# Modulation chunks beside attention: from a matrix product on TensorE to row blocks summed on VectorE and GpSimd

## The chip, the cores and the metric

The kernel runs on one NeuronCore of a Trainium2 chip. Times are device microseconds (us) of one execution. The engines are PE (TensorE; PEld is its weight load), DVE (VectorE), ACT (ScalarE), POOL (GpSimd) and SP (SyncE, which here only issues DMAs). All data are float32.

## What is computed

A diffusion backbone of two layers over 256 context tokens and 1024 latent tokens. Each layer scales, shifts and gates its activations by a modulation vector of 6 x 1024 numbers. It depends on a conditioning vector, and there are two of these: one for the context tokens and one for the latents.

```
mod_ctx = (silu(c_ctx) @ w_ada[l] + b_ada[l])[None, None, :]
xp, ckv, kpe = layer_step(xp, mod_ctx, None, None, None, p)
mod_lat = (silu(c) @ w_ada[l] + b_ada[l])[:, None, :]
xs, _, _ = layer_step(xs, mod_lat, rope, cache_ckv[:, l], cache_krope[:, l], p)

def layer_step(x, mod, rope, ctx_ckv, ctx_krope, p):
    sh1, sc1, g1, sh2, sc2, g2 = jnp.split(mod, 6, axis=-1)
    h = rmsnorm(x, p['norm1_g']) * (1 + sc1) + sh1
    mix, ckv, kpe = token_mixers(h, rope, ctx_ckv, ctx_krope, p)
    x = x + g1 * mix
    h = rmsnorm(x, p['norm2_g']) * (1 + sc2) + sh2
    x = x + g2 * expert_choice_ffn(h, p)
```

`token_mixers` holds attention (4 heads), a short convolution and a gated mixing of chunks; `expert_choice_ffn` is a mixture of 16 experts. `w_ada` is 2 x 1024 x 6144, 48 MB in all, and every number of it is read once. The change concerns `silu(c) @ w_ada + b_ada` and nothing else.

## The kernel before

**Chunks.** `w_ada` is worked in chunks of 512 columns, twelve to a layer, each a 1024 x 512 block of 2 MB that lies in the SBUF as 128 partitions x 8 row blocks (k) x 512. The first four chunks of layer 0 are done ahead of everything else. The other twenty are done inside attention: `ADA_ITEMS` names twelve for the attention of layer 0 (eight of layer 0, four of layer 1) and eight for that of layer 1.

**Attention.** One engine program each for PE, ACT and DVE walks over NI = 18 items, in two groups of nine. Each group (a pair of heads) has one item for the context tokens (items 0 and 9, called prompt items) and eight for tiles of 128 latent tokens. Iteration n of the loop computes scores of item n and finishes item n-1:
- PE: `scores` (L890) and `rotary_scores` (L902) of item n; `turn` (L939), four transposes of the exponents of item n-1 into PSUM bank 6; `times_values` (L957, or L954 for a prompt item); `turn_out` (L973). The order is written out by hand.
- DVE: `copy_turned` (L1636) takes each four transposes out of bank 6, six times per iteration (twice where item n-1 is a prompt item); PE may not refill bank 6 before it has. In between stand `invert_sum` (L1645), `scale_out` (L1657) and `row_max` (L1623, then L1627) for both heads of the pair.
- ACT: `exponents` (L1331) and `copy_out` (L1343).

In the text, copy (s, r) is `copy_turned` of head s, round r, so that an iteration has copies (0,0), (0,1), (0,2), (1,0), (1,1), (1,2). A slot m is the place for a chunk in iteration m+1.

**A chunk inside attention.** Chunk i stands in slot i, that is one in each of the first iterations. In the iteration, ahead of the last `times_values`, PE does `modulation` (L915): `cond` holds the two conditions in 2 of 32 columns, and for each of 8 row blocks and 4 column blocks of 128 there is one product with a 128x32 stationary block, 32 instructions. The sum stands in four row groups of bank 6. DVE adds the bias (`bias_modulation`, L1679), PE turns the result (`turn_modulation`, L924), and DVE copies it into `mod_all` (`copy_modulation`, L1688). The bias step waits until PE has summed and comes after `row_max(n, 1)` in DVE's order. The next transposes into bank 6 wait for the copy.

**Transfers.** The weights of a chunk alternate between two of the three 2 MB slots of `ring` (`ada_w[i % 2]`: slots 2 and 0). SP issues the load of chunk i (L505, and four small bias loads L507) once the bias step of chunk i-2 is done. Four chunks (`ADA_GATES`) are also stored to DRAM by POOL, eight small DMAs each (L602). Apart from these POOL has nothing to do until attention ends. `W_OUT`, the weights of the output projection (L1059), goes into the same two ring slots after the last two chunks are summed.

## Time and profile before

| | us |
|---|---|
| median of 3 runs | 2655.22 (2654.74 to 2655.59) |
| profiled execution, its time | 2650.42 |
| its span in the trace | 2648.7 |
| attention of layer 0, about | 340 to 662 |
| attention of layer 1, about | 1633 to 1950 |
| PE busy | 2418.7 (91%) |
| DVE busy | 799.2 (30%) |
| POOL busy | 224.9 (8%) |

The profile is of one execution. The busy times say how much an engine did, not what set the end; that is read from the chain of waits and, inside attention, from the order in time. A row of the timeline gives start, duration, engine, line and operation, and in brackets how long the engine sat idle before it and what ended that. A PE instruction on float32 has two records. Matmul ends are modelled and weight loads overlap matmuls, so that distances between starts are better read than ends.

### The profile page before, as it was taken

The page shows a single profiled execution, that of the slowest core. Times are in us where ns is not written, and L with a number is a line of the kernel's source. Part 1 is how long each engine was busy: PE and PEld are TensorE (multiplying, and loading weights), DVE is VectorE, ACT ScalarE, POOL GpSimd, SP SyncE. Part 2 cuts the span into 40 slices and gives each one's busy share as a digit, 9 for nine tenths or more (in the row PEclk, how much of TensorE's full clock was granted, in tenths as well). Part 3 has the DMA queues.
Part 4 walks back from the last instruction along what each step waited for, and adds up shares of the span by engine and source line. Part 5 has one row for each costly group of instructions (what it writes and reads, how often), then busy time and mean ns, then how long its engine had stood idle before and what let it go on. Part 6 is the DMA issues. An engine that isn't in the chain of part 4 may idle for free.

```text
span 2648.7 us, 33684 instructions
## 1 busy us (share of the span) xinstructions
PE 2418.7 (91%) x13939; PEld 1624.9 (61%) x13939; DVE 799.2 (30%) x1694; ACT 490.0 (18%) x985; POOL 224.9 (8%) x357
## 2 busy tenths in 40 slices
PE   3999999999995699999979999999999929999994
PEld 2545566666442587878745455676654418787873
DVE  1401344454235311111132023444533351111112
ACT  2410121122233011010142002122213401001012
POOL 1000010100000112121200000010000001212120
PEclk8999999999998799999989999999999959999997
DMA  8100213311234388888840003330023238888886
GB/s 298 43 0 20 80 66 127 129 64 42 78 122 151 123 268 280 278 269 276 276 142 16 20 0 98 110 118 11 1 90 111 88 119 263 281 277 270 275 280 232
DMA packets 164733, 383.64 MB, mean 145 GB/s; under 512 B 14610, under 2 KB 25116, under 8 KB 164636
## 3 DMA queue, kind: packets, MB, share of 16 engines
q1 hardware_dynamic: 145180, 332.68, 36.7%
q0 software_dynamic: 19456, 49.59, 7.4%
q8 instruction: 70, 1.15, 0.2%
q14 instruction: 27, 0.22, 0.0%
HBM read 334.63 MB, written 47.61 MB: 144 GB/s over the span
## 4 chain that ended last, share of the span: by engine, by line
PE 90%; DVE 5%; DMA 2%; SPq 1%; ACT 1%; issue 1%; DVEq 0%; POOL 0%; POOLq 0%; ACTq 0%
PE PS L1193 11%; PE PS L1200 11%; PE PS L1059 10%; PE PS L1220 9%; PE PS L797 8%; PE PS L957 7%; PE PS L890 6%; PE PS L751 5%; PE PS L740 5%; PE PS L939 4%; PE PS L902 4%; PE PS L1214 2%; PE PS L851 1%; PE PS L915 1%; PE PS L1178 1%; DVE top_i L1789 1%
## 5 line engine op out<-in xcount | busy, mean ns | idle before, releaser
L1193 PEld LDWEIGHTS PS<-r,ring 128*128 128x128 f32 x2048 | 285.8, 192 | 18.6 <-issue 18.6
L1193 PE MATMUL PS<-r,ring 128*128 128x160 f32 x2048 | 288.0, 302 | 3.4 <-ACT r L1436 3.4
L1059 PE MATMUL PS<-ring,mix 128*128 128x512 f32 x640 | 287.3, 603 | 1.2 <-DVE mix L1666 1.2
L1200 PE MATMUL PS<-r,ring 128*128 128x160 f32 x2048 | 283.4, 299 | 0.0
L1200 PEld LDWEIGHTS PS<-r,ring 128*128 128x128 f32 x2048 | 279.9, 190 | 0.0
L1220 PE MATMUL PS<-ring,r 128*128 128x512 f32 x512 | 228.3, 599 | 0.0
L890 PE MATMUL PS<-lat,r 128*128 128x512 f32 (+1 forms) x416 | 205.5, 579 | 5.4 <-ACT r L1316 2.7
L797 PE MATMUL PS<-r,ring 128*128 128x512 f32 (+1 forms) x576 | 208.4, 521 | 1.6 <-ACT r L1273 1.6
L1059 PEld LDWEIGHTS PS<-ring,mix 128*128 128x128 f32 x640 | 120.2, 193 | 140.8 <-issue 140.7
L957 PE MATMUL PS<-r 128*128 128x128 f32 x1536 | 202.2, 276 | 0.0
L957 PEld LDWEIGHTS PS<-r 128*128 128x128 f32 x1536 | 188.1, 192 | 18.9 <-issue 18.7
L1861 DVE TENSOR_TENSOR r<-r,PS 128x320 f32<-128x320 f32 x64 | 31.2, 488 | 505.0 <-PE PS L1200 505.0
L1636 DVE COPY r<-PS 128x512 f32<-128x512 f32 x200 | 138.3, 692 | 136.4 <-PE PS L939 135.2
L797 PEld LDWEIGHTS PS<-r,ring 128*128 128x128 f32 x576 | 109.1, 190 | 100.6 <-issue 95.0
L1220 PEld LDWEIGHTS PS<-ring,r 128*128 128x128 f32 x512 | 94.6, 190 | 120.3 <-issue 120.3
L939 PEld LDWEIGHTS PS<-ident,r 128*128 128x128 f32 x800 | 92.8, 141 | 105.5 <-issue 81.3
L1331 ACT ACTIVATE r<-PS,nmax 128x1536 f32<-128x1536 f32 x64 | 98.6, 1540 | 228.8 <-DVE nmax L1627 184.2
L751 PE MATMUL PS<-ring,r 128*128 128x512 f32 x320 | 140.0, 592 | 0.0
L939 PE MATMUL PS<-ident,r 128*128 128x128 f32 x800 | 122.2, 275 | 5.8 <-DVE r L1636 3.5
L740 PE MATMUL PS<-ring,r 128*128 128x448 f32 x320 | 123.9, 540 | 0.3 <-ACT r L1249 0.3
L1436 ACT ACTIVATE r<-PS,mod_all,scale_all 128x128 f32<-128x128 f32 x136 | 51.1, 456 | 376.1 <-PE PS L1178 376.1
L1447 ACT ACTIVATE r<-PS 128x320 f32<-128x320 f32 x64 | 24.5, 435 | 485.4 <-PE PS L1193 485.4
(254 smaller groups left out, 2199.1 us busy)
## 6 DMA issues: line engine op xcount, KB each, us to landing
ring<-in_w_gate_dram SPq DMA_DIRECT2D x32, 2048.0 KB, 9.9
ring<-in_w_up_dram SPq DMA_DIRECT2D x32, 2048.0 KB, 10.3
ring<-in_w_down_dram SPq DMA_DIRECT2D x32, 2048.0 KB, 9.5
ring<-in_w_ada_dram SPq DMA_DIRECT2D x21, 2048.0 KB, 22.9
x_dram<-r SPq DMA_DIRECT2D x20, 512.0 KB, 2.8
r<-x_dram SPq DMA_DIRECT2D x20, 512.0 KB, 4.1
ring<-in_w_in_dram SPq DMA_DIRECT2D x4, 2048.0 KB, 11.3
r<-in_x_sample_dram SPq DMA_DIRECT2D x16, 512.0 KB, 4.3
```

The source lines that it names most:

```text
L740: ins = pe.matmul(psum(4 + t % 2, 448), hT[:, k, t * P:(t + 1) * P], W_IN[0][:, k, :], start=(k == 0), stop=(k == KD - 1))
L751: ins = pe.matmul(psum(t % 4, 512), hT[:, k, t * P:(t + 1) * P], W_IN[1][:, k, :], start=(k == 0), stop=(k == KD - 1))
L797: ins = pe.matmul(psum(base + j, tn), W_IN[u][:, k, c0:c0 + P], hT[:, k, t0:t0 + tn], start=(k == 0), stop=(k == KD - 1))
L890: ins = pe.matmul(psum(3 * slot + c, w), QA[:, 2 * ITEMS[n][0] + slot, q], CKV[:, keys], start=(slot == 0), stop=(slot == 1))
L902: ins = pe.matmul(psum(3 * slot + c, w), QP[rows, ITEMS[n][0], q], KR[rows, keys], start=(slot == 1), stop=(slot == 0))
L939: ins = pe.transpose(PS[:, 6, j * P:(j + 1) * P], Pr[slot][:, (4 * r + j) * P:(4 * r + j + 1) * P], ident[:, :])
L957: ins = pe.matmul(PS[:, 7, slot * 256:slot * 256 + P], PTr[slot][:, k, :], CKVT[:, PT + k, :], start=(k == 0), stop=(k == 11))
L1059: ins = pe.matmul(psum(2 * (s % 2) + n, 512), mix[:, k, s * P:(s + 1) * P], W_OUT[n][:, k, :], start=(k == 0), stop=(k == KD - 1))
L1193: ins = pe.matmul(PS[:, b // 2, (b % 2) * 256:(b % 2) * 256 + SLOTS], W_G[:, k, b * P:(b + 1) * P], XST[par][:, k, :], start=(k == 0), sto ...
L1200: ins = pe.matmul(PS[:, 2 + b // 2, (b % 2) * 256:(b % 2) * 256 + SLOTS], W_U[:, k, b * P:(b + 1) * P], XST[par][:, k, :], start=(k == 0), ...
L1220: ins = pe.matmul(psum(4 + n, 512), HID[:, k, 0:CAP_S], W_D[:, k, n * 512:(n + 1) * 512], start=(k == 0), stop=(k == 3))
L1636: dve.tensor_copy(PTr[slot][:, 4 * r:4 * r + 4, :], psum(6, 512).rearrange("p (k q) -> p k q", q=P))\
```

## The change

- A chunk's product is split. For the context condition (g = 0) DVE sums, for the latent condition (g = 1) POOL sums: over the 8 row blocks k, acc[g] += c_t[:, column of (g, k)] * w[:, k, :], elementwise on 128 x 512. What is left to do is the sum over the 128 partitions, and PE does it with a stationary block `pick` that has ones in column g: 2 x 4 products in place of 8 x 4.
- DVE does 8 instructions per chunk, one TENSOR_SCALAR and seven SCALAR_TENSOR_TENSOR, placed between the copies of the iteration in which PE sums the chunk. POOL does 15, eight TENSOR_SCALAR and seven TENSOR_TENSOR, each waiting for the one before, as early as the weights have landed and chunk i-2 has been summed.
- The accumulators and a scratch row lie in `lat[:, 0:2560]`, where the query latents were; POOL waits for the last reader of these (`qa_summed`).
- The chunks no longer stand in one iteration after another. `ADA_SLOT` spreads them: slots 1, 2, 3, 5, 6, 8, 9, 10, 12, 13, 15, 16 in layer 0, and 1, 3, 5, 7, 9, 11, 13, 15 in layer 1. With them move the bias step, the transpose and copy, the loads and the loads of `W_OUT`.
- POOL's stores of chunk i come after its sums of chunk i+1.
- Two semaphores are dropped by merging them with others (`wrs_ready`, `ident_zero`).

```diff
+ADA_SLOT = [{i * (NI - 1) // len(items) + 1: i for i in range(len(items))} for items in ADA_ITEMS]
...
-        cond = r1[:, 9472:9728].rearrange("p (k c) -> p k c", k=KD)
+        pick = r1[:, 9472:9536].rearrange("p (g c) -> p g c", g=2)
+        scaled = lat[:, 2048:2560]
+        acc = [[lat[:, 1024 * i + 512 * g:1024 * i + 512 * (g + 1)] for g in range(2)] for i in range(2)]
...
-                for i, (la, n) in enumerate(ADA_ITEMS[l]):
+                def accumulate(i):
+                    before = (ADA_AT[l] + i) * (2 * KD - 1)
+                    pool.wait_ge(ada_landed[i % 2], 80 * ((ADA_AT[l] + i) // 2 + 1))
+                    if i >= 2:
+                        pool.wait_ge(ada_summed, ADA_AT[l] + i - 1)
+                    a = acc[i % 2][1]
+                    for k in range(KD):
+                        if k:
+                            pool.wait_ge(acc_pool, before + 2 * k - 1)
+                        pool.tensor_scalar(scaled if k else a, ada_w[i % 2][:, k, :], c_t[:, KD + k:KD + k + 1], None, ALU.mult)                            .then_inc(acc_pool, 1)
+                        if k:
+                            pool.wait_ge(acc_pool, before + 2 * k)
+                            pool.tensor_tensor(a, a, scaled, ALU.add).then_inc(acc_pool, 1)
...
+                pool.wait_ge(qa_summed, at(l, HEADS, HEADS))
+                for i in range(len(ADA_ITEMS[l])):
+                    accumulate(i)
+                    if i:
+                        store_gate(i - 1)
+                store_gate(len(ADA_ITEMS[l]) - 1)
...
-                    pe.wait_ge(ada_landed[i % 2], 80 * ((ADA_AT[l] + i) // 2 + 1))
-                    pe.wait_ge(pt_ready, at(l, ROUNDS, turned(i, 1, rounds_of(i) - 1)))
-                    for k in range(KD):
+                    pe.wait_ge(acc_pool, (ADA_AT[l] + i + 1) * (2 * KD - 1))
+                    pe.wait_ge(acc_dve, (ADA_AT[l] + i + 1) * KD)
+                    pe.wait_ge(pt_ready, at(l, ROUNDS, turned(m, 1, rounds_of(m) - 1)))
+                    for g in range(2):
                         for j in range(4):
-                            ins = pe.matmul(PS[32 * j:32 * j + 32, 6, 0:P], cond[:, k, :],
-                                            ada_w[i % 2][:, k, P * j:P * (j + 1)], start=(k == 0), stop=(k == KD - 1))
+                            ins = pe.matmul(PS[32 * j:32 * j + 32, 6, 0:P], pick[:, g, :], acc[i % 2][g][:, P * j:P * (j + 1)],
+                                            start=(g == 0), stop=(g == 1))
...
+                def accumulate(m, k0, k1):
...
+                    for k in range(k0, k1):
+                        w, col = ada_w[i % 2][:, k, :], c_t[:, k:k + 1]
+                        if k == 0:
+                            ins = dve.tensor_scalar(a, w, col, None, ALU.mult)
+                        else:
+                            dve.wait_ge(acc_dve, (ADA_AT[l] + i) * KD + k)
+                            ins = dve.scalar_tensor_tensor(out=a, in0=w, scalar=col, in1=a, op0=ALU.mult, op1=ALU.add)
```

On DVE, the stretch of an iteration of layer 0 from copy (0,0) to the first `row_max` reads before (here iteration 8, which holds chunk 7):

```order
L1636 COPY r<-PS 128x512 [waits o_summed,p_turned] x3
L1645 RECIPROCAL pinv<-psum_row 128x1 [waits exp_done]
L1657 TENSOR_SCALAR r<-PS,pinv 128x128 [waits o_turned,o_summed,dve_own]
L1636 COPY r<-PS 128x512 [waits o_summed,p_turned] x2
L1623 TENSOR_REDUCE pmax<-PS 128x1 [waits summed0]
```

and now, in an iteration that holds a chunk (here iteration 7, slot 6, chunk 4):

```order
L1669 COPY r<-PS 128x512 [waits o_summed,p_turned]
L1728 TENSOR_SCALAR lat<-ring,c_t 128x512 [waits ada_summed,ada_landed0]
L1669 COPY r<-PS 128x512 [waits o_summed,p_turned]
L1731 SCALAR_TENSOR_TENSOR lat<-ring,c_t,lat 128x512 [waits acc_dve]
L1669 COPY r<-PS 128x512 [waits o_summed,p_turned]
L1731 SCALAR_TENSOR_TENSOR lat<-ring,c_t,lat 128x512 [waits acc_dve]
L1678 RECIPROCAL pinv<-psum_row 128x1 [waits exp_done]
L1731 SCALAR_TENSOR_TENSOR lat<-ring,c_t,lat 128x512 [waits acc_dve,dve_own]
L1731 SCALAR_TENSOR_TENSOR lat<-ring,c_t,lat 128x512 [waits acc_dve] x3
L1690 TENSOR_SCALAR r<-PS,pinv 128x128 [waits o_turned,o_summed]
L1669 COPY r<-PS 128x512 [waits o_summed,p_turned]
L1731 SCALAR_TENSOR_TENSOR lat<-ring,c_t,lat 128x512 [waits acc_dve]
```

The copies and the scaling are the same; the eight sums stand between them, five of them in one run ahead of the scaling L1690.

On POOL, from the clearing of the bias rows to the loads of the gates, where before there were only stores:

```order
L595 MEMSET r 128x128 [waits conv_summed]
L596 MEMSET r 128x128
L602 DMA mod_dram<-r 16x1x8 [waits ada_biased]
L602 DMA mod_dram<-r 16x1x8 x7
L602 DMA mod_dram<-r 16x1x8 [waits ada_biased]
L602 DMA mod_dram<-r 16x1x8 x7
```

now the sums of the next chunk come ahead of each store (the last product and sum of chunk 1, the stores of chunk 0, the start of chunk 2):

```order
L611 TENSOR_SCALAR lat<-ring,c_t 128x512 [waits acc_pool]
L614 TENSOR_TENSOR lat<-lat 128x512 [waits acc_pool]
L623 DMA mod_dram<-r 16x1x8 [waits ada_biased]
L623 DMA mod_dram<-r 16x1x8 x7
L611 TENSOR_SCALAR lat<-ring,c_t 128x512 [waits ada_summed,ada_landed0]
L611 TENSOR_SCALAR lat<-ring,c_t 128x512 [waits acc_pool]
L614 TENSOR_TENSOR lat<-lat 128x512 [waits acc_pool]
```

Each of POOL's sums waits for the one before it.

On PE, at the end of an iteration with a chunk, before:

```order
L890 MATMUL PS<-lat,r 128x512
L957 MATMUL PS<-r 128x128 x4
L915 MATMUL PS<-ring,r 32x128 x32
L957 MATMUL PS<-r 128x128 x4
L924 MATMUL PS<-ident,r 128x128
```

and now:

```order
L918 MATMUL PS<-lat,r 128x512
L988 MATMUL PS<-r 128x128 x4
L945 MATMUL PS<-lat,r 32x128 x8
L988 MATMUL PS<-r 128x128 x4
L955 MATMUL PS<-ident,r 128x128
```

The place is the same; 32 instructions have become 8.

## Rows read from the trace of the kernel before

**Rows 1.** The page: engines' busy time, the chain that ended last by engine.
```profile
PE 2418.7 (91%) x13939; PEld 1624.9 (61%) x13939; DVE 799.2 (30%) x1694; ACT 490.0 (18%) x985; POOL 224.9 (8%) x357
...
PE 90%; DVE 5%; DMA 2%; SPq 1%; ACT 1%; issue 1%; DVEq 0%; POOL 0%; POOLq 0%; ACTq 0%
```

**Rows 2.** Groups by line, layer 0's attention: records, busy us, mean ns, idle.
```profile
L915 PE MATMUL PS<-ring,r 128*32 128x128 f32 x768 | 23.5, 274 | 0.0
```

**Rows 3.** Timeline, ends of iterations with a chunk: start, us, engine, line.
```profile
357.48 0.28 DVE L1679 TENSOR_TENSOR r<-PS,r 128x128 f32<-128x128 f32 x1
357.82 0.14 PEld L924 LDWEIGHTS PS<-ident,r 128*128 128x128 f32 x1 [0.69 <-DVE r L1679]
...
374.18 1.95 PE L915 MATMUL PS<-ring,r 128*32 128x128 f32 x64
375.40 0.15 DVE L1627 TENSOR_SCALAR nmax<-pmax 128x1 f32<-128x1 f32 x1
376.07 1.16 PE L957 MATMUL PS<-r 128*128 128x128 f32 x8
376.20 0.29 DVE L1679 TENSOR_TENSOR r<-PS,r 128x128 f32<-128x128 f32 x1 [0.65 <-PE PS L915]
376.52 0.39 SPq L505 DMA_DIRECT2D ring<-in_w_ada_dram  x1
376.95 0.14 PEld L924 LDWEIGHTS PS<-ident,r 128*128 128x128 f32 x1
378.67 0.69 DVE L1636 COPY r<-PS 128x512 f32<-128x512 f32 x1 [0.92 <-PE PS L939]
...
397.55 0.69 DVE L1636 COPY r<-PS 128x512 f32<-128x512 f32 x1 [0.92 <-PE PS L939]
```

**Rows 4.** Timeline, DVE in an iteration without a chunk, and the next one's first copy.
```profile
610.34 0.69 DVE L1636 COPY r<-PS 128x512 f32<-128x512 f32 x1 [0.64 <-PE PS L939]
611.85 0.69 DVE L1636 COPY r<-PS 128x512 f32<-128x512 f32 x1 [0.81 <-PE PS L939]
614.04 0.69 DVE L1636 COPY r<-PS 128x512 f32<-128x512 f32 x1 [1.50 <-PE PS L939]
619.03 0.35 DVE L1657 TENSOR_SCALAR r<-PS,pinv 128x128 f32<-128x128 f32 x1 [4.23 <-PE PS L957]
619.40 0.69 DVE L1636 COPY r<-PS 128x512 f32<-128x512 f32 x1
620.91 0.69 DVE L1636 COPY r<-PS 128x512 f32<-128x512 f32 x1 [0.81 <-PE PS L939]
...
627.04 0.69 DVE L1636 COPY r<-PS 128x512 f32<-128x512 f32 x1 [0.64 <-PE PS L939]
```

**Rows 5.** Groups by line and shape, DVE: elementwise work from SBUF to SBUF.
```profile
L1507 DVE TENSOR_SCALAR r<-r,rstd 128x1024 f32<-128x1024 f32 x20 | 15.1, 754 | 0.7
L1583 DVE SCALAR_TENSOR_TENSOR r<-mix,vec_all,r 128x1023 f32<-128x1023 f32 x4 | 5.1, 1278 | 0.0
L1583 DVE SCALAR_TENSOR_TENSOR r<-mix,vec_all,r 128x255 f32<-128x255 f32 x4 | 1.9, 484 | 0.1
```

**Rows 6.** Groups by line and shape, POOL: one input, and waits between.
```profile
L636 POOL COPY r<-r 128x256 f32 x32 | 12.8, 400 | 484.3 <-PE PS L1178 484.3
L570 POOL TENSOR_SCALAR_AFFINE_SELECT sel<-sel 128x16 f32<-128x16 f32 x4 | 0.8, 196 | 0.4
```

**Rows 7.** Stretches after the load at 376.52: us, engines, PEclk, DMA share, GB/s.
```profile
383.00:384.00 1.00, 1.00 (x6) 0.52 (x7) 0.12 (x2) 0.00 (x0) 0.00 (x0) 1.00 0.78 270
384.00:385.00 1.00, 1.00 (x8) 0.41 (x6) 0.00 (x0) 0.00 (x0) 0.00 (x0) 1.00 0.00 0
```

**Rows 8.** Timeline, DVE where a prompt item is finished (layer 0, iteration 1).
```profile
347.74 0.61 DVE L1657 TENSOR_SCALAR r<-PS,pinv 128x128 f32<-128x128 f32 x2 [1.25 <-PE PS L954]
351.89 0.69 DVE L1636 COPY r<-PS 128x512 f32<-128x512 f32 x1 [3.54 <-PE PS L939]
```

**Rows 9.** Timeline: the first products with `W_OUT` in layer 0.
```profile
662.86 7.11 PE L1059 MATMUL PS<-ring,mix 128*128 128x512 f32 x16 [0.61 <-DVE mix L1666]
```

More of the change, by code:

```diff
@@ L289, in backbone @@
         ada_summed = sem("ada_summed")
+        acc_dve = sem("acc_dve")
+        acc_pool = sem("acc_pool")
         ada_biased = sem("ada_biased")
@@ L935, in turn @@
                         pe.wait_ge(o_copied, at(l, NI, n))
-                    if slot == 0 and r == 0 and 0 < n <= len(ADA_ITEMS[l]):
-                        pe.wait_ge(ada_copied, ADA_AT[l] + n)
+                    if slot == 0 and r == 0 and n - 1 in ADA_SLOT[l]:
+                        pe.wait_ge(ada_copied, ADA_AT[l] + ADA_SLOT[l][n - 1] + 1)
                     for j in range(4):
@@ L1605, in rotate @@
                     dve.tensor_tensor(x, x, SHUF, ALU.add).then_inc(qp_ready, 1)
-                condition(cond)
+                step(dve.memset(pick, 0.0))
+                for g in range(2):
+                    ins = dve.tensor_scalar(pick[:, g, g:g + 1], ones[:, 0:1], 1.0, None, ALU.mult)
+                ins.then_inc(cond_ready, 1)
                 dve.wait_ge(wa_summed, at(l, 1, 1))
@@ L1666, in copy_value_heads, with bias_modulation @@
                     dve.tensor_copy(mix[:, h, t0:t0 + tn], psum(m % 6, tn)).then_inc(uvh_copied[1], 1)
-                def bias_modulation(i):
-                    if i < 0 or i >= len(ADA_ITEMS[l]):
+                def bias_modulation(m):
+                    i = ADA_SLOT[l].get(m)
+                    if i is None:
                         return
-                    stored = [ADA_AT[m] + k for m in range(DEPTH) for k, (_, n) in enumerate(ADA_ITEMS[m])
-                              if n in ADA_GATES and ADA_AT[m] + k <= ADA_AT[l] + i - 2 and k % 2 == i % 2]
+                    stored = [ADA_AT[q] + k for q in range(DEPTH) for k, (_, n) in enumerate(ADA_ITEMS[q])
+                              if n in ADA_GATES and ADA_AT[q] + k <= ADA_AT[l] + i - 2 and k % 2 == i % 2]
                     if stored:
@@ L1679, in bias_modulation, with copy_modulation @@
                     dve.tensor_tensor(ada_s[i % 2], psum(6, P), ada_b[i % 2], ALU.add).then_inc(ada_biased, 1)
-                def copy_modulation(i):
-                    if i < 0 or i >= len(ADA_ITEMS[l]):
+                def accumulate(m, k0, k1):
+                    i = ADA_SLOT[l].get(m)
+                    if i is None:
+                        return
+                    a = acc[i % 2][0]
+                    if k0 == 0:
+                        dve.wait_ge(ada_landed[i % 2], 80 * ((ADA_AT[l] + i) // 2 + 1))
+                        if i >= 2:
+                            dve.wait_ge(ada_summed, ADA_AT[l] + i - 1)
+                    for k in range(k0, k1):
[5 more added lines that the diff above has]
+                            ins = dve.scalar_tensor_tensor(out=a, in0=w, scalar=col, in1=a, op0=ALU.mult, op1=ALU.add)
+                        ins.then_inc(acc_dve, 1)
+                def copy_modulation(m):
+                    i = ADA_SLOT[l].get(m)
+                    if i is None:
                         return
@@ L1698, in _ @@
                 for n in range(NI):
-                    for r in range(3):
-                        copy_turned(n - 1, 0, r)
+                    copy_turned(n - 1, 0, 0)
+                    accumulate(n - 1, 0, 1)
+                    copy_turned(n - 1, 0, 1)
+                    accumulate(n - 1, 1, 2)
+                    copy_turned(n - 1, 0, 2)
+                    accumulate(n - 1, 2, 3)
                     invert_sum(n - 1, 0)
+                    accumulate(n - 1, 3, 7)
                     scale_out(n - 1, 0)
                     copy_turned(n - 1, 1, 0)
+                    accumulate(n - 1, 7, 8)
                     copy_turned(n - 1, 1, 1)
```

29 lines of the change are left out of this document (15 added, 14 removed).

## The prediction

> **What bounds the kernel now.** I read the page first. PE is busy 91% of the span and carries 90% of the chain that ended last [rows 1]. So work taken off PE counts, as far as PE does not then wait for others. The chunks stand in two attention stages. There I read the order in time, since what matters is which wait ends last within one iteration. Two distances give the frame. From first copy to first copy an iteration with a chunk takes 397.55 - 378.67 = 18.88 us [rows 3], and one without takes 627.04 - 610.34 = 16.70 us [rows 4]. A chunk costs 2.18 us of the path, twenty chunks 43.6 us; no form of this change can save more. PE has no long idle stretch in either. But PE fills bank 6 six times per iteration, and DVE must empty it each time: where rows 4 show DVE idle before a copy, it waits for PE, and where it shows no idle (copy (1,0) at 619.40, right behind the scaling), the two are level. The next transposes wait for the copy, so a DVE that is late at a copy makes PE late by the same amount.
>
> **PE's part.** The 64 records of L915 take 376.07 - 374.18 = 1.89 us from their start to the next instruction's [rows 3]; twelve chunks have 768 records and 23.5 us [rows 2], so all chunks are alike. A quarter of the instructions is left, of the same shape: 0.47 us. That saves 1.42 us a chunk. The bias step gives part of it back. Before, it waits 0.65 us for PE [rows 3], then ends at 376.49, well ahead of the transpose at 376.95. Now PE reaches the transpose at 376.95 - 1.42 = 375.53, while DVE is at `row_max` and its follower until 375.55. The bias step ends at 375.86, and with 0.05 us for the signal PE starts at 375.91: a new wait of 0.38 us. Left are 1.42 - 0.38 = 1.04 us a chunk, **20.8 us** for twenty.
>
> **DVE's eight sums, alone.** TENSOR_SCALAR from SBUF to SBUF takes 0.754 us on 1024 elements [rows 5]; with the small fixed part of such instructions I take 0.41 us for 512. SCALAR_TENSOR_TENSOR takes 1.278 us on 1023 and 0.484 us on 255 [rows 5], 1.03 ns an element, so 0.75 us on 512, and 0.03 us for the wait on its predecessor. Against the idle times of rows 4: k=0 (0.41) lies in 0.81 us; k=1 (0.78) in 1.50; k=2 to 6, five of them, 3.9 us with their waits and starts 4.05, in the 4.23 before the scaling; k=7 (0.78) in 0.81. All is covered, but the cover of the run of five has 0.2 us to spare and that of k=7 0.03. Alone these sums cost nothing. Any lengthening of them goes to PE almost in full. One slot of each layer (slot 9) finishes a prompt item, where DVE's idle before the scaling is only 1.25 us and before the next copy 3.54 [rows 8]: seven sums of 5.1 us against 4.8, and k=7 pushes `row_max`; I take 0.8 us each, **1.6 us**.
>
> **POOL's fifteen.** No row shows POOL with two inputs. With one input it takes 0.292 us on 128 elements and 0.196 on 16, 0.86 ns an element; the copy of 256 in 0.400 fits this [rows 6]. One input on 512: 0.62 us. Two inputs: not under 0.62; 0.18 + 2 x 0.44 = 1.06 if a second read is added to the first; 0.18 + 3 x 0.44 = 1.50 if the write then no longer overlaps either. I take 1.20, nearer to the 1.06. Waits between two instructions of POOL are 0.1 us (0.4 over four) [rows 6]. Sum per chunk: 8 x 0.62 + 7 x 1.20 + 15 x 0.1 = 14.9 us. The Trainium skill (GPSIMD Engine Reference, performance versus the Vector engine) gives 4497 ns for a two-input add of 2048 elements, from which about 1.24 us on 512 would be an estimate; it leaves the sum as it is.
> Is POOL in time? The load at 376.52 has ended by 384 [rows 7], 8 us after the bias step that releases it. So POOL starts on chunk i+2 about 8 us after the bias step of chunk i and ends at 23 us alone. The least distance between these two slots is two iterations, 35 us. PE does not wait for POOL, also not if DVE stretches POOL's work by 8 x 0.75 = 6 us. The first two chunks landed before attention. DVE's own wait for landing, 20 us after the release at the least, is covered too.
>
> **The two together.** Both engines now work from SBUF to SBUF at the same time, DVE on instructions with one or two SBUF inputs, POOL in a nearly unbroken row. No row of before shows this pair side by side. The bounds of what it adds to one DVE sum: nothing, or a wait for the instruction that POOL has under way. With two instructions waiting in turns, that is POOL's mean, (0.62 + 1.20) / 2 = 0.91, less the 0.03 that DVE waits anyway: 0.88 us. The rows don't settle it. I take the upper end, because DVE's one-input form runs at 0.74 ns an element and so must move more than one element per step of 1.03 ns, and its two-input form fetches two [rows 5]: either needs a second way into SBUF, and POOL's work needs one as well. The Trainium skill (SBUF — State Buffer, on the shared port pair) states this outright: a VectorE instruction with two SBUF inputs, or in a 2-port mode, and a GpSimd instruction that reads SBUF exclude each other for the whole of an instruction. By that rule the change pays the sum below; were the pair independent it would be the rival below. No run here shows it yet.
> Where do they meet? POOL starts on a chunk 8 us after a bias step, which is 5.7 us into the next iteration (the bias step ends 2.2 us before the first copy [rows 3]); DVE's k=4 starts some 6 us into an iteration. So:
> - Slot 1 of each layer: POOL is on chunk 1 throughout. Five sums wait: 4.4 - 0.2 = 4.2 us, and k=7 0.85. 5.1 us, twice.
> - Slot 12 of layer 0: POOL, held up by the stores of chunks 6 and 7 (3.9 us each), is on the next chunk nearly throughout: 4.5 us.
> - Slots 2, 6, 13 directly after another slot: k=4 to 7 wait, 2.9 us each. Slot 10 behind the prompt slot 9: 3.6. Slot 9 of layer 1, where seven sums stand in a row, 2.7 beyond its 0.8.
> - Slot 3: 1.3; slots that follow an empty one (5, 8, 15 in layer 0; 3, 5, 7, 11, 13 in layer 1): POOL is on its last instructions, 0.6 each.
> Sum: 10.2 + 4.5 + 8.7 + 3.6 + 2.7 + 1.3 + 4.8 = **35.8 us**.
>
> **What costs nothing.** The loads of `W_OUT` move from the eleventh and twelfth iteration to the sixteenth and seventeenth; the last chunk is summed at about 639 and the second half is needed 3.5 us after 662.86 [rows 9], against 8 us of transfer. The stores of the gates and `scale2` are ready long before attention ends. `pick` is shorter to build than `cond`. The merged semaphores come out where nothing waited.
>
> **The sum.** -20.8 + 1.6 + 35.8 = +16.6 us on the profiled execution: 2650.4 + 16.6 = 2667.0. The median of the runs lies 4.8 us above that execution; I carry the difference over: 2655.2 + 16.6 = **2672**.
> This case has its own spread. With 0.62 us for POOL's two-input form and shorter meetings the waits shrink to some 8 us, and the time is 2643; with 1.50 they grow to some 55, and it is 2691.
>
> **The rivals.**
> 1. DVE and POOL don't hinder each other. For it: no row shows that they do, and eight sums fit DVE's idle times as if measured for it. Then -20.8 + 1.6 = -19.2 us: 2636. It needs the 1.04 us per chunk to hold; if the bias step's wait of 0.38 us vanished it would be 2629, and if half the gain went into waits at copies that are level, 2646.
> 2. POOL is the bound (slower, on the other side, also without hindrance). In slots two apart POOL has 35 - 8 = 27 us for its fifteen, of which 15 are used. Should its instructions take over 1.8 us on average instead of 0.89, PE waits at `modulation`, with all behind it: twelve chunks in 16 iterations of 17.5 us leave 23 us a chunk, load included for every second; at 2 us an instruction (30 us a chunk) layer 0 alone would take (30 - 23) x 12 = 84 us more, 2720 and above. Against it: POOL's rows would have to be twice too short.
> 3. The hindrance is there but POOL gives way (DVE is served first), or only one of the instruction kinds is concerned. Then half of 35.8 is paid or less: about 2650 to 2655, no difference to be seen.
>
> **How the numbers follow.** A measurement of this kernel can tell about 0.2%, 5.3 us, from no change. The forecast (hindered in turns) has 0.50; rival 1 0.33; rival 2 0.05; rival 3 0.12. Faster by over 0.2% (under 2649.9): rival 1 nearly whole, 0.31, a sixth of the forecast's low end, 0.05, a little of rival 3: 0.38. Same: 0.14. Slower by over 0.2%: 0.48. The range must take in rival 1 at 2636 and the forecast's upper bound of 2691: 2633 to 2692. The forecast's own range is 2648 to 2691.
>
> **What would show each step.** PE: the products at L945 take 0.47 us a chunk, and the transpose at L955 waits some 0.4 us for the bias step. DVE: L1731 has a shortest duration near 0.75 us; if the hindrance is real, its longest is 1.5 us or more, and these stand only where POOL is busy; L1728 is 0.41 at its shortest. POOL: L611 near 0.62 and L614 near 1.2, and longer where DVE sums. Iterations: 17.8 us with a chunk and no POOL work beside it, above 20 with. PE's idle time before transposes that DVE's copies release grows in slots 1, 2, 6, 10, 12, 13 of layer 0 and hardly in layer 1, whose attention should be about level with before. I am wrong if L1731 is the same everywhere (then rival 1), or if PE's wait at L945 is for POOL (rival 2).

## The result, and the profile after

| | before | after |
|---|---|---|
| median of 9 runs, us | 2653.40 (2652.21 to 2655.59) | 2662.89 (2658.74 to 2666.82) |
| time of the profiled execution, us | 2650.4 | 2659.95 |
| layer 0's attention, first to last rotary scores, us | 290.65 | 296.70 |
| layer 1's attention, the same, us | 282.82 | 282.99 |

The changed kernel takes 1.0035 of the time of the one before [1.0025 to 1.0045]: slower by 9.5 us. The forecast was 2672, slower by 17 than the 2655.2 from which it started; against that base the measured kernel is 7.7 slower. The sign came out, the size is about half, and the loss sits in layer 0 as forecast. The changed kernel's runs also lie wider apart (8 us) than those of before (3 us).

The page of the changed kernel, with the lines that answer to [rows 1]:

```profile
PE 2399.8 (90%) x12979; PEld 1602.5 (60%) x12979; DVE 948.1 (36%) x1856; ACT 489.7 (18%) x985; POOL 677.0 (25%) x657
...
PE 79%; DVE 8%; POOL 6%; DMA 2%; issue 2%; SPq 1%; ACT 1%; DVEq 0%; POOLq 0%; ACTq 0%
```

PE has 960 matmuls less and is 18.9 us less busy. But its share of the chain falls from 90% to 79%, and POOL, which had none, has 6%, DVE 8%. POOL carries 452 us more of work than before. The chain names lines of POOL: somewhere PE waits for POOL itself, which the prediction had excluded.

Groups by line of the changed kernel, from the page (count | busy us, mean ns | idle before and its releaser):

```profile
L611 POOL TENSOR_SCALAR lat<-ring,c_t 128x512 f32<-128x512 f32 x160 | 266.8, 1667 | 120.6 <-PE PS L879 62.8
...
L614 POOL TENSOR_TENSOR lat<-lat 128x512 f32<-128x512 f32 x140 | 185.6, 1326 | 11.7
...
L1731 DVE SCALAR_TENSOR_TENSOR lat<-ring,c_t,lat 128x512 f32<-128x512 f32 x140 | 145.8, 1042 | 3.3 <-DVE pinv L1678 0.4
```

The same lines asked for one by one, and DVE's first instruction of a chunk (L1728); the three durations are shortest, median and longest in ns:

```profile
L611 POOL TENSOR_SCALAR lat<-ring,c_t x160: 1561/1563/2110, 338.4 to 1878.3; 128x512 f32<-128x512 f32 x160
...
L614 POOL TENSOR_TENSOR lat<-lat x140: 1259/1267/1800, 341.7 to 1880.2; 128x512 f32<-128x512 f32 x140
...
L1731 DVE SCALAR_TENSOR_TENSOR lat<-ring,c_t,lat x140: 734/989/1750, 360.0 to 1912.3; 128x512 f32<-128x512 f32 x140
...
L1728 DVE TENSOR_SCALAR lat<-ring,c_t x20: 476/520/1443, 358.5 to 1903.2; 128x512 f32<-128x512 f32 x20
```

Two readings. DVE's sum has its forecast length at the shortest (734 ns; forecast 0.75 us) and is mostly longer: the hindrance is real. And the POOL instruction that has only one large input takes 1.56 us, longer than the one with two (1.26). The prediction had 0.62 for the first, from [rows 6], and 1.20 for the second. (The 0.292 us on 128 elements that it names is a select of the same kind at L565 and not among rows 6; the two rows shown there, 16 in 0.196 and 256 in 0.400, give the same 0.85 ns an element and 0.62 us.) Fifteen instructions come to 8 x 1.56 + 7 x 1.26 + 15 x 0.09 = 22.7 us a chunk, not 14.9. DVE's one-input L1728 is 0.48 at its shortest (forecast 0.41), and it too is lengthened, up to 1.44.

How one meeting looks, in the changed kernel's first iteration with a chunk (start, us, engine, line):

```profile
360.96 3.66 POOL L611 TENSOR_SCALAR lat<-ring,c_t 128x512 f32<-128x512 f32 x2
...
363.08 4.77 DVE L1731 SCALAR_TENSOR_TENSOR lat<-ring,c_t,lat 128x512 f32<-128x512 f32 x4
...
364.70 1.50 POOL L614 TENSOR_TENSOR lat<-lat 128x512 f32<-128x512 f32 x1
366.30 1.88 POOL L611 TENSOR_SCALAR lat<-ring,c_t 128x512 f32<-128x512 f32 x1
...
368.03 0.67 DVE L1669 COPY r<-PS 128x512 f32<-128x512 f32 x1
368.27 1.27 POOL L614 TENSOR_TENSOR lat<-lat 128x512 f32<-128x512 f32 x1
368.63 1.45 DVE L1731 SCALAR_TENSOR_TENSOR lat<-ring,c_t,lat 128x512 f32<-128x512 f32 x1
...
368.85 0.63 PE L970 MATMUL PS<-ident,r 128*128 128x128 f32 x4 [0.75 <-DVE r L1669]
```

The sum at 368.63 starts 0.36 us after POOL's two-input addition and ends at 370.08, 0.54 after that one's end at 369.54. Its own length is 0.74, so it was held for 0.71 us, until about 0.2 before the end of the addition's record. POOL is lengthened as well (1.50 and 1.88 instead of 1.26 and 1.56). The copy behind the run of four is late, and PE waits 0.75 us for it. The copies themselves, out of PSUM, keep their 0.67 to 0.69.

### The profile page after: what moved, and what is told of

It is laid out like the page before. It is cut to its first block, busy times and chain, and to the rows that moved or that the text cites. A ratio compares the mean times of both kernels' runs of the same rounds, so it can differ in the third digit from the quotient of the medians.

```text
span 2658.2 us, 32280 instructions
## 1 busy us (share of the span) xinstructions
PE 2399.8 (90%) x12979; PEld 1602.5 (60%) x12979; DVE 948.1 (36%) x1856; ACT 489.7 (18%) x985; POOL 677.0 (25%) x657
## 4 chain that ended last, share of the span: by engine, by line
PE 79%; DVE 8%; POOL 6%; DMA 2%; issue 2%; SPq 1%; ACT 1%; DVEq 0%; POOLq 0%; ACTq 0%
PE PS L1223 11%; PE PS L1230 10%; PE PS L1090 10%; PE PS L1250 9%; PE PS L825 8%; PE PS L779 5%; PE PS L768 5%; PE PS L988 4%; PE PS L918 4%; POOL lat L611 3%; PE PS L970 3%; PE PS L1244 2%; POOL lat L614 2%; DVE lat L1731 2%; PE PS L930 1%
## 5 line engine op out<-in xcount | busy, mean ns | idle before, releaser
L611 POOL TENSOR_SCALAR lat<-ring,c_t 128x512 f32<-128x512 f32 x160 | 266.8, 1667 | 120.6 <-PE PS L879 62.8
L614 POOL TENSOR_TENSOR lat<-lat 128x512 f32<-128x512 f32 x140 | 185.6, 1326 | 11.7
L970 PEld LDWEIGHTS PS<-ident,r 128*128 128x128 f32 x800 | 93.1, 141 | 121.9 <-issue 102.9
L1731 DVE SCALAR_TENSOR_TENSOR lat<-ring,c_t,lat 128x512 f32<-128x512 f32 x140 | 145.8, 1042 | 3.3 <-DVE pinv L1678 0.4
L970 PE MATMUL PS<-ident,r 128*128 128x128 f32 x800 | 122.7, 276 | 22.4 <-DVE r L1669 20.7
```

The source lines that it names most:

```text
L611: pool.tensor_scalar(scaled if k else a, ada_w[i % 2][:, k, :], c_t[:, KD + k:KD + k + 1], None, ALU.mult) .then_inc(acc_pool, 1)
L614: pool.tensor_tensor(a, a, scaled, ALU.add).then_inc(acc_pool, 1)
L970: ins = pe.transpose(PS[:, 6, j * P:(j + 1) * P], Pr[slot][:, (4 * r + j) * P:(4 * r + j + 1) * P], ident[:, :])
L1731: ins = dve.scalar_tensor_tensor(out=a, in0=w, scalar=col, in1=a, op0=ALU.mult, op1=ALU.add)
```

## The experiments

Four theories are to be told apart: the two engines hinder each other in turns (the forecast); DVE's sums are simply too much for its idle time; POOL is too slow and PE waits for it; the new slots of the chunks are worse. All times are medians; "the kernel before" is always the one timed on the same chip in the same job.

### The changed kernel again, and its parts one at a time

Unchanged, for the same chip:

> The changed kernel again, beside the runs that follow. Both theories: about 9 us over the kernel before (0.2 to 0.5%).

2660.73 against 2653.56, 1.0026 [1.0016, 1.0037]: +7.2 us. The parts are to add up to this.

PE's part: both engines stop after the first row block.

```diff
-                    for k in range(KD):                  # POOL
+                    for k in range(1):
...
-                    for k in range(k0, k1):              # DVE
+                    for k in range(k0, min(k1, 1)):
```

> Leaves out the sums over row blocks 1 to 7 on both engines: one DVE and one POOL instruction a chunk are left, with PE's eight products, the spread slots and all waits. It measures PE's part alone. My working gave -20.8 us against the kernel before (1.04 us a chunk); a chunk iteration of 17.8 us against 16.70 without. A rival, that the bias step's wait or the spread slots eat the gain, expects -10 us or less.

2630.50, 0.9912 [0.9899, 0.9926]: **-23.1 us**. From its timeline:

```profile
372.80 0.65 PE L945 MATMUL PS<-lat,r 128*32 128x128 f32 x16
...
373.38 1.16 PE L988 MATMUL PS<-r 128*128 128x128 f32 x8
...
374.10 0.28 DVE L1713 TENSOR_TENSOR r<-PS,r 128x128 f32<-128x128 f32 x1
...
374.43 0.33 PE L955 MATMUL PS<-ident,r 128*128 128x128 f32 x1
```

The products take 373.38 - 372.80 = 0.58 us up to the next instruction (forecast 0.47). The bias step ends at 374.38 and the transpose L955 starts at 374.43, those 0.05 us later with which the forecast reckoned; the view shows no idle time in front of it (forecast 0.38). An iteration with a chunk takes 17.74 us from rotary scores to rotary scores, 18.89 before: 1.15 a chunk, times 20 is 23.0. The products alone would leave 1.42 - 0.11 = 1.31, so 0.16 us a chunk go elsewhere, and the only candidate in sight is a short wait at L955 that the modelled end of the matmul before it covers. That is not shown.

DVE's sums complete, POOL's still one row block:

```diff
-                    for k in range(KD):                  # POOL
+                    for k in range(1):
```

> DVE does all its eight sums, POOL only its first instruction of fifteen (seven eighths of one condition's sum are left out). Theory that only the meeting of DVE and POOL costs: within 3 us of the run without sums, at most 1.6 us for the two prompt slots above it, and L1731 at 0.73 to 0.76 us everywhere. Rival, that DVE's eight sums alone overfill its idle times: 5 us or more above the run without sums.

2633.18, 0.9921 [0.9908, 0.9935]: **+2.7** over the last. Its group, against the 1042 ns above:

```profile
L1731 DVE SCALAR_TENSOR_TENSOR lat<-ring,c_t,lat 128x512 f32<-128x512 f32 x140 | 106.4, 760 | 3.3 <-DVE pinv L1678 0.4
```

Nearly all iterations stay at 17.74. In the profiled executions one alone grows: that of slot 8 of layer 0 (scores of prompt item 9) takes 13.93 in place of 12.85, since the run of four sums makes the copy behind it late. The iterations of slot 9 do not grow. "DVE has too little idle time" falls. An ordinary slot shows what cover there is (the same kernel's timeline):

```profile
362.87 3.11 DVE L1731 SCALAR_TENSOR_TENSOR lat<-ring,c_t,lat 128x512 f32<-128x512 f32 x4
366.56 0.35 DVE L1690 TENSOR_SCALAR r<-PS,pinv 128x128 f32<-128x128 f32 x1 [0.58 <-PE PS L988]
```

0.58 us are left behind the run of sums, where the prediction had 0.2.

POOL's complete, DVE's one row block:

```diff
-                    for k in range(k0, k1):              # DVE
+                    for k in range(k0, min(k1, 1)):
```

> POOL does all fifteen, DVE only its first (seven eighths of the other condition's sum are left out). Theory of hindrance in turns: POOL undisturbed takes 8 x 1.56 + 7 x 1.27 + waits, some 22 us a chunk, and PE waits for it at one place or none; the time lies within 5 us of the run without sums. Rival, that POOL's slow instructions alone make the loss: PE waits at its chunk products in several slots, and the time comes near that of the changed kernel.

2637.31, 0.9936 [0.9923, 0.9950]: **+6.8** over PE's part alone, more than the 5 us that were allowed for. Who PE waits for at its products (us, times):

```profile
L945 PE MATMUL PS<-lat,r x320: 269/273/297, 373.5 to 1893.6; 128*32 128x128 f32 x160
...
  POOL lat L614: 9.6, 7
```

So POOL is late by itself, at seven products and not at one or none as expected, above all in layer 0: the iteration of slot 3 takes 21.64 and that of slot 13 takes 19.14 instead of 17.74. In layer 1, where the slots are two apart, no iteration grows by more than 0.2 us.

The parts add up so: -23.1 + 2.7 + 6.8 = -13.6; measured +7.2. The difference, **20.7 us**, is there only when DVE's and POOL's sums run together. This is the hindrance's part, forecast at 35.8. Most of it shows as PE's waits for DVE's copies: before its transposes L970 PE waits 3.1 us for `copy_turned` in the kernel with PE's part alone, 4.2 with DVE's sums, 3.1 with POOL's and 21.1 with both, 16.9 more than with DVE's alone. PE's wait for POOL at L945 grows from 10.4 to 12.4, because DVE lengthens POOL's instructions. The clock (below) can hold 3.4 us at most. These are sums of waits in single executions, and they overlap; they need not add up to 20.7 exactly.

### Which of POOL's instructions hinder

Writes alone: all fifteen of POOL's instructions replaced by fills of the same tiles.

```diff
-                        pool.tensor_scalar(scaled if k else a, ada_w[i % 2][:, k, :], c_t[...], None, ALU.mult)
+                        pool.memset(scaled if k else a, 0.0)
...
-                            pool.tensor_tensor(a, a, scaled, ALU.add)
+                            pool.memset(a, 0.0)
```

> POOL's fifteen instructions a chunk become fifteen that write zeros to the same rows and read nothing (the latent condition's sums are left out); DVE's eight are complete. Theory that a two-input DVE instruction is held up by what POOL reads: L1731 stays at 0.73 to 0.76 us throughout and the time is that of the run with DVE's sums alone, 2633 us. Rival, that any POOL work in SBUF holds DVE up: L1731 has a mean over 0.85 us and the time is 2636 or more.

2632.51, 0.9919 [0.9902, 0.9935]: level with DVE's sums alone. Groups by line:

```profile
L1731 DVE SCALAR_TENSOR_TENSOR lat<-ring,c_t,lat 128x512 f32<-128x512 f32 x140 | 104.7, 748 | 3.3 <-DVE pinv L1678 0.4
...
L611 POOL MEMSET lat<- 128x512 f32 x160 | 83.9, 524 | 292.6 <-DMA r<-in_b_ada_dram 221.8 <-PE PS L879 62.7
```

A POOL that only writes costs DVE nothing.

The scalings alone (eight a chunk), and the additions alone (eight a chunk, of row blocks as they are):

```diff
-                        pool.tensor_scalar(scaled if k else a, ...)
-                            pool.tensor_tensor(a, a, scaled, ALU.add)
+                        pool.tensor_scalar(a, ada_w[i % 2][:, k, :], c_t[...], None, ALU.mult)   # scalings alone
...
+                        pool.tensor_tensor(a, a, ada_w[i % 2][:, k, :], ALU.add)                 # additions alone
```

> DVE's eight sums complete, POOL's seven additions left out, so that only its eight TENSOR_SCALAR (one SBUF input, 1.56 us) are left. Read from the changed kernel's rows: a DVE sum that starts 0.5 us or more after such an instruction is let through by 0.8 us after its start, so the wait is 0.3 us at most. Theory: the mean of L1731 rises by under 0.15 us and the time stays within 3 us of the run with DVE's sums alone (about 2633 to 2636). Theory of full turns, as in the prediction: DVE waits the rest of 1.56 us, mean above 1.1 us, 2640 or more.

> DVE's eight sums complete, POOL does eight TENSOR_TENSOR a chunk (two SBUF inputs, the product left out) and no TENSOR_SCALAR. Theory: two-input instructions of both engines exclude each other for their whole length; DVE sums beside POOL take 1.3 to 1.7 us. POOL is busy only 8 x 1.27 = 10 us a chunk, half as long as in the changed kernel, but with every instruction of the kind that blocks: 5 to 12 us above the run with DVE's sums alone (2638 to 2645). If it stays at 2633 to 2636 the kind of POOL's instruction does not matter.

Scalings alone 2633.05, 0.9919 [0.9903, 0.9936]; additions alone 2645.23, 0.9969 [0.9959, 0.9978], against the same 2654.14. Groups by line, first of the scalings' kernel, then of the additions':

```profile
L1728 DVE SCALAR_TENSOR_TENSOR lat<-ring,c_t,lat 128x512 f32<-128x512 f32 x140 | 109.6, 783 | 3.3 <-DVE pinv L1675 0.4
...
L611 POOL TENSOR_SCALAR lat<-ring,c_t 128x512 f32<-128x512 f32 x160 | 253.7, 1586 | 239.1 <-DMA r<-in_b_ada_dram 163.1 <-PE PS L876 62.8
```
```profile
L1730 DVE SCALAR_TENSOR_TENSOR lat<-ring,c_t,lat 128x512 f32<-128x512 f32 x140 | 117.3, 838 | 3.3 <-DVE pinv L1677 0.4
...
L611 POOL TENSOR_TENSOR lat<-lat,ring 128x512 f32<-128x512 f32 x140 | 183.2, 1309 | 11.0
```

The scalings are 254 us of POOL's work and cost the kernel nothing beyond DVE's own sums (2633.05; DVE's sums alone 2633.18). The additions are 210 us of work (with the first of each chunk, on a line of its own) and cost 12. POOL has less to do in both kernels and meets fewer of DVE's 140 sums, so the meetings have to be counted in the traces (mean length of a sum that starts while POOL has such an instruction under way):

| kernel | inside a scaling | inside an addition |
|---|---|---|
| scalings alone | 42 sums, 0.86 us | |
| additions alone | | 18 sums, 1.45 us |
| the changed kernel | 77 sums, 0.87 us | 47 sums, 1.41 us |

Eighteen meetings with additions cost the kernel 12 us, forty-two with scalings nothing. So it is above all POOL's two-input instruction that hinders. That both engines read the same weights is not the reason: in the changed kernel the additions read `lat` alone, and the scalings, which read `ring` as DVE does, hinder less. In the timeline of the scalings' kernel a sum within an unbroken row of six scalings takes 1.14 us, another 0.74, and a run of four 3.42 (3.11 alone):

```profile
355.10 10.28 POOL L611 TENSOR_SCALAR lat<-ring,c_t 128x512 f32<-128x512 f32 x6
...
360.15 1.14 DVE L1728 SCALAR_TENSOR_TENSOR lat<-ring,c_t,lat 128x512 f32<-128x512 f32 x1
...
362.34 0.74 DVE L1728 SCALAR_TENSOR_TENSOR lat<-ring,c_t,lat 128x512 f32<-128x512 f32 x1
...
363.19 3.42 DVE L1728 SCALAR_TENSOR_TENSOR lat<-ring,c_t,lat 128x512 f32<-128x512 f32 x4
```

### Are the new slots the cause?

The product of before with its 32 instructions (64 records), no sums, in the changed kernel's slots:

```diff
-                    if i < 0 or i >= len(ADA_ITEMS[l]):
+                    i = ADA_SLOT[l].get(m)
+                    if i is None:
```

> The kernel before, its product on PE unchanged, with the chunks in the spread slots of the changed kernel. Theory that the spreading is free: within 3 us of the kernel before. Rival, that the spreading accounts for part of PE's 23 us gain (the first slot of each layer moves from a prompt item into a full iteration): 3 us or more faster.

2652.85 against 2653.51, 0.9995 [0.9985, 1.0004]. For PE's product the slots by themselves cost and bring nothing. What three slots in a row do to a slow POOL is another matter (above).

### A shorter instruction for POOL

The scaling with a constant instead of the column (so its sums are not those of the kernel), and the scaling as a two-input product with the column spread over the row:

```diff
-   pool.tensor_scalar(..., c_t[:, KD + k:KD + k + 1], None, ALU.mult)
+   pool.tensor_scalar(..., 0.5, None, ALU.mult)                                        # constant
...
+   pool.tensor_tensor(..., c_t[:, KD + k:KD + k + 1].to_broadcast([P, 512]), ALU.mult) # spread column
```

> The changed kernel with the constant 0.5 in POOL's TENSOR_SCALAR in place of the column of the condition (the latent modulation is then not the reference's). If the column operand makes the 1.56 us, it falls to the 0.62 us that I had worked out from POOL's copy; if the instruction is that slow in itself, it stays.

> The changed kernel with POOL's scaling by TENSOR_TENSOR, the column read as a broadcast input, in place of TENSOR_SCALAR; the output is complete. If POOL's TENSOR_SCALAR at 1.56 us is slow by its form, the replacement takes 1.26 us, POOL needs 2.4 us less a chunk, its lateness (6.8 us) mostly goes, and the meeting with DVE shrinks: 2653 to 2657 us. If the form makes no difference: 2661.

The constant takes 0.07 us off the 1.56: fetching the column is not what makes the scaling slow. What does is open. One execution of that kernel took 2658.19. Line L611 of it:

```profile
L611 POOL TENSOR_SCALAR lat<-ring x160: 1482/1489/1952, 339.9 to 1875.2; 128x512 f32<-128x512 f32 x160
```

The spread column took POOL's scaling down to 1.04 us at the median, but the kernel not down to the expected 2653 to 2657: it went up to **2686.49**, 1.0114 [1.0096, 1.0131]: some 26 us above the changed kernel, with a POOL that is 86 us less busy in this line. Its groups:

```profile
L1731 DVE SCALAR_TENSOR_TENSOR lat<-ring,c_t,lat 128x512 f32<-128x512 f32 x140 | 159.1, 1136 | 3.3 <-DVE pinv L1678 0.4
...
L611 POOL TENSOR_TENSOR lat<-ring,c_t 128x512 f32<-128x512 f32 x160 | 180.8, 1130 | 192.5 <-DMA r<-in_b_ada_dram 118.7 <-PE PS L879 62.8
```

The mild instruction was replaced by one of the kind that holds DVE up; the mean sum is 94 ns longer, 13 us over 140 sums, and PE's wait for copies before its transposes is 38.6 us against 21.1 in the repeat of the changed kernel. PE's wait for POOL at L945 falls from 12.4 to 0.8, for which the spread column was meant. The windows over the two attention stages (us, then PE, PEld, DVE, ACT, POOL, granted clock, DMA share, GB/s) show what goes with it; first this kernel, then the changed kernel, then the kernel before:

```profile
335.00:660.00 325.00, 296.19 (x1768) 195.71 (x1767) 237.76 (x368) 63.38 (x95) 239.76 (x212) 0.96 0.21 72
1615.00:1935.00 320.00, 293.93 (x1662) 192.15 (x1661) 207.87 (x310) 69.04 (x99) 161.30 (x146) 0.98 0.18 63
```
```profile
335.00:660.00 325.00, 299.78 (x1846) 197.95 (x1844) 242.60 (x386) 66.94 (x102) 290.87 (x219) 0.99 0.24 83
1615.00:1935.00 320.00, 304.45 (x1799) 198.82 (x1798) 213.56 (x341) 70.97 (x103) 196.41 (x153) 1.00 0.20 67
```
```profile
335.00:660.00 325.00, 318.13 (x2465) 216.24 (x2464) 154.81 (x296) 68.68 (x105) 18.94 (x39) 1.00 0.25 87
1615.00:1935.00 320.00, 312.98 (x2184) 208.59 (x2183) 153.54 (x278) 70.60 (x105) 18.97 (x39) 1.00 0.19 64
```

The granted clock is 1.00 in both stages in the kernel before and has a mean of 0.96 and 0.98 here. In the finer clock records of the traces that is 23.9 us at 1.2 GHz in layer 0's attention and 13.7 in layer 1's, against 6.8 and none in the changed kernel (10.2 and none in its repeat). At half the rate this can cost at most half of the difference to the repeat, 13.7 us. The three parts, 17.5 - 11.6 + 13.7 = 19.6 at most, leave some 6 of the 26 us open.

### Without POOL

If the pair is the trouble, DVE alone should win what its idle time holds. Half: DVE's eight instructions sum row blocks 0 to 3 for both conditions, PE multiplies blocks 4 to 7 as before (16 products) and adds the two sums (8).

```diff
+                    for k in range(KD // 2, KD):
+                        for j in range(4):
+                            pe.matmul(PS[...], cond[:, k, :], ada_w[i % 2][:, k, P * j:P * (j + 1)], ...)
...
+                        g, q = k % 2, k // 2
+                        a = acc[i % 2][g]
+                        w, col = ada_w[i % 2][:, q, :], c_t[:, KD * g + q:KD * g + q + 1]
```

> No sums on POOL. DVE's eight instructions sum row blocks 0 to 3 for both conditions, PE does row blocks 4 to 7 as before and then adds the two sums over the partitions: 24 products a chunk. Theory (DVE's sums cost only where they meet POOL): PE saves 8 of 32 products, 0.47 us a chunk, and the bias step needs no new wait: -8 to -11 us against the kernel before. Rival (moving work to DVE costs by itself): no difference.

2647.09, 0.9978 [0.9967, 0.9988]: -6.4 us, faster but short of the 8 to 11 expected. An iteration with a chunk takes 18.45 us, 0.44 less than before; that of slot 8 in layer 0 takes 14.44, 0.29 more than with before's product in the same slots.

Then all sixteen sums on DVE for the eleven chunks whose preceding iteration holds none, eight in each of the two iterations, with PE's part as in the changed kernel; the other nine as just described:

```diff
-                        return
+                        i = ADA_SLOT[l].get(m + 1)
+                        if i is None or m < 1:
+                            return
+                    elif i in ADA_FULL[l]:
+                        k0, k1 = k0 + 8, k1 + 8
```

> No sums on POOL. Where the iteration ahead of a chunk's holds no chunk (four of twelve in layer 0, seven of eight in layer 1), DVE does eight instructions there and eight in the chunk's own, all row blocks for both conditions, and PE only its eight adding products; for the other nine chunks DVE and PE halve the work as in the run before. Theory: DVE's idle times are free as long as POOL reads nothing, so these eleven chunks gain 1.15 us each as in the run without sums and the nine some 0.35: 14 to 17 us under the kernel before, about 2638. Rival, that sixteen sums lengthen the path: 2645 or more.

2638.14 against 2653.84, **0.9944** [0.9931, 0.9958]: 15.7 us faster than the kernel before, where the changed kernel is 9.5 slower. Its group by line:

```profile
L1745 DVE SCALAR_TENSOR_TENSOR lat<-ring,c_t,lat 128x512 f32<-128x512 f32 x208 | 147.1, 745 | 1.1
```

DVE does 208 of the long sums instead of 140, each in 745 ns instead of 1042: nearly the same busy time (147.1 us against 145.8; records that overlap count once) holds half as much again.

## Where the prediction held and where it failed

Term by term, in the repeated run and its parts: PE -23.1 instead of -20.8, DVE alone +2.7 instead of +1.6, POOL's lateness +6.8 instead of nothing, the two together +20.7 instead of +35.8. The sum is +7.2 instead of +16.6. The step that put the size off is the last term, and the one left out is the wait for POOL. Without that wait the two kernels would by these sums be level (+0.4): that the change came out slower at all rests on a term which the forecast had ruled out, so its right sign is partly luck.

**PE's part: right.** -20.8 forecast, -23.1 measured. Two small misses nearly cancel: the products end 0.11 us later than a quarter of the old time, and of the new wait of 0.38 at most the 0.16 above is there. In the changed kernel PE waits 0.37 us at 375.45, where DVE is late.

**DVE alone: the number right, the place wrong.** +1.6 forecast, +2.7 measured, with L1731 at 0.74 to 0.75 as forecast. But the forecast had it as 0.8 in slot 9 of each layer. There the iterations are as long as without sums (16.57 in both layers); the cost that shows is 1.08 us in slot 8 of layer 0, which had no term. That the sum was near is luck.

**POOL's fifteen: wrong, and with it "PE does not wait for POOL".** "One input on 512: 0.62 us" was 1.56. The elements were priced by a copy and a select; the scaling by a column runs at another rate, and neither row told it. The other value, 1.20 for two inputs, was 1.26, though it was the less certain. By the Trainium skill (GPSIMD Engine Reference, performance versus the Vector engine), whose figure the prediction turned into an estimate of about 1.24, the trace agrees for the addition (1.26 us); the remark on the same page of the Trainium skill (engine selection) that one-input work runs at roughly line rate does not hold for this scaling (1.56 us, against 0.48 for L1728, DVE's instruction of the same form). From 22.7 us a chunk, and longer where DVE sums, "PE does not wait for POOL" fell too. In the changed kernel, at slot 3:

```profile
412.39 1.26 POOL L614 TENSOR_TENSOR lat<-lat 128x512 f32<-128x512 f32 x1
...
413.70 0.94 PE L945 MATMUL PS<-lat,r 128*32 128x128 f32 x16 [2.49 <-POOL lat L614]
```

POOL worked on this chunk from 389.43 to 413.65, 24.2 us, because the chunk before it and the stores of a gate (3.95 us) had kept it until then. Rival 2 had this mechanism and its test ("if PE's wait at L945 is for POOL"), with a threshold of 1.8 us an instruction from slots on average. The slots are not average: three in a row (1, 2, 3) exhaust POOL's lead at 1.4 us already (8 x 1.56 + 7 x 1.26 over fifteen), as the kernel with POOL's sums alone shows at slot 3 (21.64 us). That is 6.8 us of the result, which had no place in the sum.

**The two together: the hindrance is there, the term mis-sized.** This is the step that failed in size: each meeting was priced at a full wait of 0.88 us. 35.8 forecast, 20.7 measured. Iterations with a chunk, longer than in the kernel with PE's part alone, from the starts of the rotary scores:

| slots | forecast, us | measured, us |
|---|---|---|
| slot 1 of layer 0 / layer 1 | 5.1 / 5.1 | 1.20 / 1.20 |
| 2, 6, 12, 13 of layer 0 | 2.9, 2.9, 4.5, 2.9 | 1.02, 1.55, 0.65, 1.56 |
| 3 of layer 0 | 1.3 | 4.92 (3.90 with POOL alone) |
| 8 to 10 of layer 0 together | 5.0 | 6.18 (0.63 with POOL alone) |
| 5, 15 of layer 0 | 0.6, 0.6 | 1.27, 1.33 |
| 3, 5, 7, 11, 13 of layer 1 | 0.6 each | 1.38, 0.84, 0.83, 1.57, 0.83 |
| 9 of layer 1 | 3.5 | 1.98 |
| sum | 37.4 | 28.3 |

The forecast's sum is 35.8 with the 1.6 of DVE alone; the measured one holds the parts of DVE and of POOL alone too. In the repeated run the single slots differ (slot 1 of both layers 0.2, slot 3 7.3, slot 13 2.7) and their sum is 28.9, so the table says how the cost is spread and not what one slot costs. The forecast paid much in a few slots and little in the others; the chip takes something in nearly every one: leaving out slot 3 and slots 8 to 10, 0.65 to 1.98, 1.2 on average. Both factors were off, in opposite ways. *Where they meet*: POOL needs 22.7 us for a chunk, so it is at work beside nearly all of DVE's sums (126 of 140), not beside some. *What a meeting costs*: the mean sum is longer by 1042 - 760 = 282 ns, not by 880. A long wait is paid only inside the two-input addition, as at 368.63 above (+0.71); inside the scaling, which is over half of POOL's time, a sum takes 0.74 to 1.21. The low price of POOL's instructions even hid part of the error: with the measured ones the same rule would have charged (1.56 + 1.26) / 2 - 0.03 = 1.38 us a meeting, and in more slots. Over 140 sums the 282 ns are 39.5 us, not far from the 35.8 that the forecast charged to PE. But spread thinly they meet cover again and again. At 440.33 the four sums take 4.54 instead of 3.11, and DVE's idle time behind them (0.58 in the timeline above) takes part of the 1.43:

```profile
440.33 4.54 DVE L1731 SCALAR_TENSOR_TENSOR lat<-ring,c_t,lat 128x512 f32<-128x512 f32 x4
444.80 0.34 DVE L1690 TENSOR_SCALAR r<-PS,pinv 128x128 f32<-128x128 f32 x1
445.06 0.67 DVE L1669 COPY r<-PS 128x512 f32<-128x512 f32 x1
...
445.88 0.63 PE L970 MATMUL PS<-ident,r 128*128 128x128 f32 x4 [0.81 <-DVE r L1669]
```

So "any lengthening of them goes to PE almost in full" failed as well. Rival 3 ("only one of the instruction kinds is concerned", half of 35.8 or less) describes this term better than the forecast: with 17.9 for it and POOL's 6.8 on top the sum is +5.5, against +7.2 measured in the repeated run.

The rule of the Trainium skill that the prediction weighed (SBUF — State Buffer, two separate sides: a lock for the whole instruction against a GpSimd instruction that reads SBUF) agrees with the fills (no cost) and with the additions. For the scaling the measurement differs: it reads SBUF for 1.56 us, yet the runs show sums inside it of 0.74 us, and 0.86 us on average in the kernel with scalings alone.

**The forecast of the shape was partly right.** Layer 1 about level: +0.2. Iterations without POOL beside them 17.8: 17.74. Iterations with it "above 20": slot 3 (22.66), the rest at most 19.3; in the repeated run slot 13 too (20.42).

## What to carry over

Before work moves to an idle engine, price its instruction by a row of the same operation; an instruction of another name with as many inputs and elements was wrong by a factor of 2.5 here. Two engines that both have idle time may not have it at the same time: ask of each pair of instructions, not of each pair of engines, whether they hold each other up, and prefer work that one engine can spread over two iterations (0.9944 here, with half of nine chunks left on PE) to work shared by two (1.0035). An order that is tight in three places and loose on average is late in the three places.

## What the runs showed of the hardware

- On POOL, scaling 128x512 by a column took 1.56 us (1.49 by a constant), adding two such tiles 1.26, multiplying by a spread column 1.04, filling 0.52.
- DVE's two-input sum of 0.74 us takes up to 1.79 when it starts inside one of POOL's additions (additions alone; 1.45 on average), keeps 0.75 beside fills, and takes 0.86 on average inside scalings. DVE's one-input L1728 of 0.48 us goes up to 1.44. Its copies out of PSUM keep their 0.67 to 0.69, also the 149 of 200 that overlap POOL's work. POOL is lengthened too: 1.56 up to 2.11, 1.26 up to 1.80.
- Two idle times of PE of 2.5 and 3.1 us came with a lower clock. At the wait of 2.49 us at slot 3 (windows of the changed kernel, columns as above; the clock is the first number behind POOL's):

```profile
410.00:412.00 2.00, 1.21 (x9) 0.86 (x7) 1.93 (x5) 1.63 (x2) 1.90 (x2) 1.00 0.00 0
412.00:414.00 2.00, 0.30 (x11) 0.30 (x15) 0.95 (x2) 0.00 (x0) 1.92 (x3) 0.98 0.00 0
414.00:416.00 2.00, 2.00 (x21) 1.61 (x11) 0.29 (x1) 0.00 (x0) 2.00 (x5) 0.50 0.02 1
```

  0.50 is the level of 1.2 GHz: the 16 products that take 0.64 us elsewhere take 0.94. The same shows in slot 8 of layer 0, where PE waits for a copy behind four sums that take 4.54 (the window, and PE's timeline); with DVE's sums alone the wait there is 1.52 us and the clock stays at 1.00:

```profile
499.00:501.00 2.00, 1.06 (x5) 1.09 (x6) 2.00 (x3) 0.00 (x0) 1.82 (x3) 0.56 0.00 0
```
```profile
499.94 1.08 PE L970 MATMUL PS<-ident,r 128*128 128x128 f32 x4 [3.13 <-DVE r L1669]
```

  So a delay of DVE or POOL can be paid a second time in PE's clock. In attention the clock records give 10.2 us at 1.2 GHz in the repeated run, 3.4 in the kernel with POOL's sums alone and none with DVE's alone. Half of the 6.8 us of difference, 3.4 us, is the most that the clock can hold of the 20.7.
